# Three joins and one order of tiles in an odd block, and the last attention pair woven with the projection behind it

## The reference

```
z = h @ w_in; u, g = split(z)                       # odd mixer
d = multiscale_pool(u)                              # 4 groups of 512 channels, windows 2, 4, 8, 16
y = einsum("bngi,gij->bngj", d, w_grp) * scale
out = (y * silu(g)) @ w_out

logits = q @ k.T * scale + c[t] - c[s]              # forgetting attention, causal, c = cumsum(log f)
o = softmax(logits) @ v
h = h + (o * silu(g)) @ fox_w_out
```

## Time and profile before

| | us |
|---|---|
| runs | 3169.97, 3166.43, 3172.95; median 3169.97 |
| profiled execution | 3172.45 |
| its span, first to last instruction | 3170.3 |
| TensorE busy | 2962.7 (93%) |
| VectorE, GpSimd, ScalarE busy | 1746.6, 1316.3, 1088.0 |

### The profile page before, as it was taken

The page is one execution under the profiler, slowest core; times in us unless marked ns, Lnnn a source line. Parts: engine busy times, 40 slices in busy tenths (PEclk is TensorE's granted clock), DMA queues, the critical chain, the costliest instruction groups (busy, mean ns, idle before and its releaser), DMA issues.

```text
span 3170.3 us, 40111 instructions
## 1 busy us (share of the span) xinstructions
PE 2962.7 (93%) x13930; PEld 2287.7 (72%) x13930; DVE 1746.6 (55%) x2284; ACT 1088.0 (34%) x1429; POOL 1316.3 (42%) x1638
## 2 busy tenths in 40 slices
PE   5999999989999999989899999998999999997997
PEld 3688888757788777867688877776667666665775
DVE  7688999955545116534632322535555655556353
ACT  5344444342211000001332221324455555665232
POOL 2344454447644434436422324775221121211575
PEclk9999999999999999999899999999999999999999
DMA  7412222344311321113301103333222212221423
GB/s 298 161 63 64 63 76 73 114 151 162 102 49 44 116 80 37 47 39 137 107 27 34 33 27 106 96 87 131 54 47 54 48 33 48 48 34 41 140 82 111
DMA packets 113294, 258.56 MB, mean 82 GB/s; under 512 B 24624, under 2 KB 38000, under 8 KB 112384
## 3 DMA queue, kind: packets, MB, share of 16 engines
q1 hardware_dynamic: 83456, 189.43, 20.5%
q10 hardware_dynamic: 29696, 67.21, 5.9%
HBM read 223.97 MB, written 32.64 MB: 81 GB/s over the span
## 4 chain that ended last, share of the span: by engine, by line
PE 75%; DVE 11%; ACT 6%; POOL 4%; issue 3%; DMA 2%; DVEq 0%; POOLq 0%; SPq 0%; ACTq 0%
PE ps L660 20%; PE ps L661 19%; PE ps L662 19%; POOL t_wl L590 3%; PE ps L1212 2%; PE ps L1229 1%; DVE ps L2117 1%; PE ps L1027 1%; PE ps L1028 1%; PE ps L1029 1%; POOL t_wh L585 1%; DVE t_ptl L2580 1%; PE ps L1249 1%; ACT t_pr L1848 1%; DVE t_pb L2327 1%
## 5 line engine op out<-in xcount | busy, mean ns | idle before, releaser
L660 PE MATMUL ps<-t_h_hi,t_wh 128*128 128x512 f32 x2464 | 1011.6, 411 | 43.9 <-POOLq L593 13.5
L585 POOL CAST t_wh<-t_wst 128x1024 fp32r<-128x1024 f32 (+2 forms) x306 | 313.6, 1025 | 1712.1 <-PE ps L662 1538.9
L661 PE MATMUL ps<-t_h_lo,t_wh 128*128 128x512 f32 x2464 | 982.7, 399 | 0.0
L662 PE MATMUL ps<-t_h_hi,t_wl 128*128 128x512 f32 x2464 | 981.9, 398 | 0.0
L590 POOL TENSOR_TENSOR t_wl<-t_wst,t_wh 128x256 fp32r<-128x256 f32 (+2 forms) x1224 | 926.1, 787 | 24.5
L660 PEld LDWEIGHTS ps<-t_h_hi,t_wh 128*128 128x128 f32 x2464 | 467.8, 190 | 196.7 <-issue 60.5
L661 PEld LDWEIGHTS ps<-t_h_lo,t_wh 128*128 128x128 f32 x2464 | 469.0, 190 | 112.7 <-issue 8.5
L662 PEld LDWEIGHTS ps<-t_h_hi,t_wl 128*128 128x128 f32 x2464 | 467.6, 190 | 112.2
L2117 DVE SCALAR_TENSOR_TENSOR ps<-t_upad,t_vec,ps 128x1024 f32<-128x1024 f32 x224 | 275.5, 1284 | 7.1 <-DVE ps L2111 0.9
L660 PE MATMUL ps<-t_y_hi,t_wh 128*128 128x512 f32 x512 | 208.4, 407 | 21.7 <-DVEq L264 14.6
L661 PE MATMUL ps<-t_y_lo,t_wh 128*128 128x512 f32 x512 | 205.6, 402 | 0.0
(11 more groups left out here) (350 smaller groups left out, 4267.4 us busy)
## 6 DMA issues: line engine op xcount, KB each, us to landing
t_wst<-w_even_in SPq DMA_DIRECT2D x40, 512.0 KB, 3.5
t_wst<-w_ple SPq DMA_DIRECT2D x64, 320.0 KB, 2.9
t_wst<-w_even_out SPq DMA_DIRECT2D x32, 512.0 KB, 3.6
t_wst<-w_fox_in SPq DMA_DIRECT2D x32, 512.0 KB, 3.6
t_modw<-w_mod SPq DMA_DIRECT2D x6, 2048.0 KB, 16.2
t_xr<-x_d ACTq DMA_DIRECT2D x6, 2048.0 KB, 11.6
t_wst<-w_gla_in SPq DMA_DIRECT2D x24, 512.0 KB, 3.8
t_wst<-w_odd_in_a SPq DMA_DIRECT2D x16, 512.0 KB, 3.6
```

What stands on the lines that cost most here:

```text
L585: pool.tensor_copy(wh[b][:, 0:w], wst[b][:, 0:w]).then_inc(S("w_high"), 1)
L660: pe.matmul(o, w1, x1, start=start and k == 0, stop=False)
L661: pe.matmul(o, w1, x2, start=False, stop=False)
L662: last = pe.matmul(o, w2, x1, start=False, stop=stop and k == kts - 1)
```

## The change

In the odd block the tiles 4 to 11 of a group come in another order, gate 0, gate 1, group 0, group 1, then as before (`ODD_ORDER`; loads by `ODD_AT`, widths by `ODD_WIDTHS`). Three `begin` waits of TensorE go: into `oout_a` and `oout_b` it waits for y of tile 6 only (`o_y`), and takes each further step of y as it is ready (`y_ready`); into `odd_b` it waits for the last residual (`x_added`).

In the last attention window VectorE runs `add_scores` of unit i+1 ahead of `low_weights` of unit i. TensorE gets 14 contraction steps (3 matmuls each) of half tiles 0 and 1 of the output projection at steps 9 to 22 (`EARLY`, into banks 6 and 7), the last two behind the window. Their operand, half 0 of `t_yf`, is split by GpSimd (`last_pair`: 8 times a copy and a subtraction of 128x512, each once its pair is done), behind the split of the projection's first two weight tiles; SyncE issues these two loads ahead of the last `load_max`. ScalarE and VectorE split half 1 only, and ScalarE issues the load of x ahead of its copies.

```diff
+ODD_ORDER = [(0, 0), (0, 1), (1, 0), (1, 1), (0, 2), (1, 2), (0, 3), (1, 3)]
...
+        return bank(6 + t if name == "fout" and t < 2 else t % 4)
...
+    EARLY = [(0, 0), (0, 1), (0, 2), (1, 0), (0, 3), (1, 1), (0, 4), (1, 2), (0, 5), (0, 6), (1, 3), (0, 7),
+             (1, 4), (1, 5)]
+    EARLY_AT = {9 + n: x for n, x in enumerate(EARLY)}
...
                     store_max(times - 1, c)
+                    if c == 1:
+                        for j in range(2):
+                            load_tile("w_fox_out", 0, j, j * T, T, (T, T))
                     load_max(times - 1, c)
...
+        def last_pair():
+
+            for i in range(1, 9):
+                if 1 <= i <= 8:
+                    k = i - 1
+                    pool.wait_ge(S("f_y"), 4 * k + 2)
+                    pool.tensor_copy(hcol(h_hi, 0, k), hcol(yf, 0, k)).then_inc(S("yf_high"), 1)
+                    pool.wait_ge(S("yf_high"), k + 1)
+                    pool.tensor_tensor(hcol(h_lo, 0, k), hcol(yf, 0, k), hcol(h_hi, 0, k).bitcast(F32),
+                                       ALU.subtract).then_inc(S("yf_ready"), 1)
...
+        def y_ready(part, k):
+            pe.wait_ge(S("o_gs"), 8 * part + 2 + k + 1)
...
-        begin(pe, "oout_a")
-        out_phase("w_odd_out_a", None, None, "w_odd_in_b")
-        begin(pe, "odd_b")
+        pe.wait_ge(S("o_y"), 4 * 1 + 7)
+        out_phase(0, "w_odd_out_a", "w_odd_in_b")
+        pe.wait_ge(S("x_added"), 2 + KT)
         odd_groups(1)
-        begin(pe, "oout_b")
-        out_by_halves("oout_b", "w_odd_out_b", lambda c: None, (y_hi, y_lo))
+        pe.wait_ge(S("o_y"), 4 * 3 + 7)
+        out_by_halves("oout_b", "w_odd_out_b", lambda c: (lambda k: y_ready(1, k)) if c == 0 else None, (y_hi, y_lo))
...
+        def early_out(t, ks):
+
+            base = first["w_fox_out"]
+            if ks[0] == 0:
+                pe.wait_ge(S("f_g"), 8)
+                pe.wait_ge(S("w_split"), base + t + 3)
+            last = project(wbuf("w_fox_out", t), None, h_hi, h_lo, chunks=[(0, HALF, out_bank("fout", t))], ks=ks,
+                           ready=(lambda k: pe.wait_ge(S("yf_ready"), k + 1)) if t == 0 else None)
+            if ks[-1] == KT - 1:
+                last.then_inc(S("w_used"), 1)
...
+                if attend and not project_more and h in EARLY_AT:
+                    early_out(EARLY_AT[h][0], (EARLY_AT[h][1],))
...
-        begin(pe, "fout")
-        out_by_halves("fout", "w_fox_out", lambda c: lambda k: pe.wait_ge(S("yf_ready"), 8 * c + k + 1), (h_hi, h_lo))
+        early_out(1, (6, 7))
+
+        pe.wait_ge(S("f_add"), 24 * 8)
+        out_by_halves("fout", "w_fox_out", lambda c: lambda k: pe.wait_ge(S("yf_ready"), 8 * c + k + 1), (h_hi, h_lo),
+                      done=2)
...
+                if isinstance(p, int) and p == 7 and i > 1:
+                    act.wait_ge(S("f_pv"), NU * p + i - 1)
                 A(pth[x][:, 0:n], pr[x][:, 0:n], ACT.Copy).then_inc(S("f_ph"), 1)
...
-            at_least("f_pv", NU * p + i - 1)
+            if not (isinstance(p, int) and p == 7):
+                at_least("f_pv", NU * p + i - 1)
+            elif i > 1:
+
+                dve.wait_ge(S("f_pl"), 24 * p + 2 * i - 2)
...
+                    if h % 2 == 1 and not project_more and h < 23:
+                        add_scores(p, h // 2 + 1, like)
                     if h % 2 == 1:
                         low_weights(p, h // 2)
```

More of the change, by code:

```diff
@@ L32 @@
 KB = 1024
+ODD_ORDER = [(0, 0), (0, 1), (1, 0), (1, 1), (0, 2), (1, 2), (0, 3), (1, 3)]
+ODD_AT = [1024 * j for j in range(4)] + [4096 + 1536 * j + 1024 * kind for kind, j in ODD_ORDER]
+ODD_WIDTHS = [1024] * 4 + [(1024, 512)[kind] for kind, j in ODD_ORDER]
 STREAMS = [
@@ L545, in _ @@
             for half in range(passes(name)):
+                if name == "w_fox_out" and half == 0:
+                    with sp.Fori(0, times - 1) as i:
+                        for j, w in enumerate(widths):
+                            load_tile(name, i + 1, j, j * T, w, widths)
+                    continue
                 with sp.Fori(0, times) as i:
                     for j, w in enumerate(widths):
-                        load_tile(name, i, j, sum(widths[:j]) if name != "w_even_in" else EVEN_AT[j], w, widths,
+                        load_tile(name, i, j, ODD_AT[j] if name.startswith("w_odd_in") else sum(widths[:j]), w, widths,
                                   half * times * len(widths))
@@ L624, in _ @@
             for half in range(passes(name)):
+                if name == "w_fox_out" and half == 0:
+                    for j, w in enumerate(widths):
+                        split_tile(name, 0, j, w, widths, 0)
+                    pool.wait_ge(S("w_used"), first[name] + 2)
+                    last_pair()
+                    with pool.Fori(0, times - 1) as i:
+                        for j, w in enumerate(widths):
+                            split_tile(name, i + 1, j, w, widths, 0)
+                    continue
                 with pool.Fori(0, times) as i:
@@ L692, in half_added, with out_by_halves @@
             pe.wait_ge(S("r_added"), 16 * ADD[name] + t + 1)
-        def out_by_halves(name, nm, ready, operand):
+        def out_by_halves(name, nm, ready, operand, done=0):
             base = first[nm]
@@ L699, in out_by_halves @@
                     t = 8 * c + m
+                    if t < done:
+                        continue
                     if t >= 4:
@@ L974, in group @@
                     project(j % 2, slot(j), h_hi, h_lo).then_inc(S("w_used"), 1)
[L975 to L984, removed]
+                for n, (kind, j) in enumerate(ODD_ORDER):
+                    take(nm, i, 4 + n)
+                    if kind == 0:
+                        act((9, 11, 13, 14)[j])
+                        project(n % 2, slot(2 * j % 4), h_hi, h_lo).then_inc(S("w_used"), 1)
+                    else:
+                        act(10) if j == 0 else act(12) if j == 1 else yev(3 + j)
+                        if j == 0:
+                            pe.wait_ge(S("o_d"), 4 * g + 4)
+                        project(n % 2, slot((2 * j + 1) % 4), d_hi, d_lo, kts=4).then_inc(S("w_used"), 1)
             if part == 0:
@@ L1626, in group @@
                 for j in range(4):
-                    act.wait_ge(S("w_used"), w0 + 5 + 2 * j + i * 12)
+                    act.wait_ge(S("w_used"), w0 + 5 + ODD_ORDER.index((0, j)) + i * 12)
                     act.wait_ge(S("o_gs"), 4 * g + j + 1)
@@ L1910, in _ @@
         begin(act, "fout")
-        for c in range(2):
-            for k in range(KT):
-                A(hcol(h_hi, c, k), hcol(yf, c, k), ACT.Copy).then_inc(S("yf_high"), 1)
         load_x(x_d)
+        for k in range(KT):
+            A(hcol(h_hi, 1, k), hcol(yf, 1, k), ACT.Copy).then_inc(S("yf_high"), 1)
         act.wait_ge(S("yf_ready"), 16)
@@ L2342, in odd_groups @@
                 for j in range(4):
-                    dve.wait_ge(S("w_used"), w0 + 6 + 2 * j)
+                    dve.wait_ge(S("w_used"), w0 + 5 + ODD_ORDER.index((1, j)))
                     dve.wait_ge(S("o_act"), 8 * g + 13 + j)
@@ L2605, in window @@
             for h in range(24):
-                if attend and h % 2 == 0:
+                if attend and h % 2 == 0 and (project_more or h == 0):
                     add_scores(p, h // 2, like)
@@ L2643, in _ @@
         begin(dve, "fout")
-        for c in range(2):
-            for k in range(KT):
-                n = 8 * c + k + 1
-                dve.wait_ge(S("yf_high"), n)
-                TT_(hcol(h_lo, c, k), hcol(yf, c, k), hcol(h_hi, c, k).bitcast(F32), ALU.subtract)\
-                    .then_inc(S("yf_ready"), 1)
+        dve.wait_ge(S("yf_ready"), 8)
+        for k in range(KT):
+            dve.wait_ge(S("yf_high"), 9 + k)
+            TT_(hcol(h_lo, 1, k), hcol(yf, 1, k), hcol(h_hi, 1, k).bitcast(F32), ALU.subtract)\
+                .then_inc(S("yf_ready"), 1)
         out_by_halves("fout", "w_fox_out", lambda k: V("ple_norm", 8 + k), lambda: p_split(1))
```

16 lines of the change are left out of this document (7 added, 9 removed).

## The result

The changed kernel takes 3137.59 us (median of 4, 3135.76 to 3139.97) against 3171.46 of the kernel before in the same job; the ratio is 0.9896, 95% interval 0.9879 to 0.9913. It is 34 us faster where the forecast was 48: the sign holds, but the time lies outside the forecast's own range of 3115 to 3129, at the upper edge of the wide one (3108 to 3138), and it is what the rival "the window gets much longer" said (3138).

What follows compares the result with a forecast made beforehand. TensorE was taken as the bound, busy 2962.7 of 3170.3 us, so only its waits and slow-clock stretches could be won. Odd block 39 plus last pair 9 (18.5 - 1.3 - 8) gave 48 off: 3122 against the median, range 3115 to 3129.

Steps and rivals of the forecast that it cites:

- the window gets much longer: Last pair, rival: TensorE drops to its lower clock at each unit's pause; pair gives -7, total 3138; chance 0.17.
- Odd block, 39: Odd block: shorter waits and slow stretches at joins and groups win 39 us, bounds 30 to 43.
- The margin of 0.2 at the split of gate 2: Odd block, first two groups: GpSimd's split, 5.4 us, fits group tile 1's 5.6, four times; 1.0 taken off.
- Last pair, what goes, 18.5: Last pair: wait of 6.29, slow stretch of 2.4 and 9.8 of steps moved into gaps, together 18.5 us.
- x late: Output projection: x's residual ready at 13.9, half tile 4 wants it at 12.6, so 1.3 us come back.
- Window longer by 8: Last pair's window: adds ahead and the first projection step lengthen it by 8 us in all.
- the ring: Last window: low part, values, scores, add follow one another, 5.3 us per full unit against a chain of 3.9.
- The first half: Window up to low part 4: 5 to 7 us later, 6 taken, through the first projection step waiting for GpSimd.
- The second half: Window from low part 4 to low part 11: 30.4 us against 28.7, so 2 more.
- Window shorter: Last window, rival: a unit costs only VectorE's busy 2.7 us, not 3.9; 6 us less, total 3108; chance 0.12.
- Odd block in part: Odd block, rival: VectorE's chain longer, or x or gate 2's split late; 39 becomes 25, total 3136; chance 0.14.
- slower: Last pair, rival: GpSimd's eight copies and subtractions hold TensorE, 85 us in place of 18; total 3189; chance 0.02.

Runs made afterwards that it cites:

- own low buffers: Changed kernel with first two weight tiles loaded early, TensorE's scores also a unit ahead, and low parts in separate buffers: 3117.9 us, ratio 0.9835 to the kernel before.
- The kernel with adds alone: Odd block changed; in the last pair only VectorE's scores added a unit ahead, no projection steps or GpSimd copies: 3154.1 us, ratio 0.9943 to the kernel before.
- weights early: Changed kernel with the output projection's first two weight tiles asked for ahead of both stores of maxima: 3132.5 us, ratio 0.9878 to the kernel before.
- steps with weights early: Changed kernel with scores added in their old place and first two weight tiles loaded ahead of the maxima: 3125.7 us, ratio 0.9862 to the kernel before.
- x early: Changed kernel with old add order, first two weight tiles loaded early, and half 0 of x loaded during the last window: 3122.4 us, ratio 0.9844.

## Why the forecast was right and wrong, step by step

**Odd block, 39: right**, 37.2 measured (34.5 in the kernel with it alone). Joins are 17.9 by the profile and 21 by the time for 18.2, the order of tiles 19.3 and 15 for 20.9: the sum stands firmer than its two parts. The waits that stay are 1.9 and 3.3 for 1.5 and 2.7. The margin of 0.2 at the split of gate 2 held: TensorE's longest wait for GpSimd in the block is 1.8 us, as it was in the kernel before.

**Last pair, what goes, 18.5: right.** With x early and the residual ahead the tail is 17.6 shorter.

**"x late", 1.3: too small, and half of the mechanism.** The wait is 4.0 us and followed by matmuls of 0.80 us. The load of x started 5.3 us behind the last values as forecast (5), but landed 9.6 later and not 8.2, which by the working above makes 3 of the 4.0. The last 1 is a wait that the forecast did not have: residual 0 is queued behind eight low parts of half 1 on VectorE, 8.8 us. The change had moved the eight of half 0 away but left these in front, while TensorE now arrives early. Each of the two hides behind the other, so taking x away alone gave 1.9; both together are worth 5 of the 17 (tail 227.1 with own low buffers, 221.9 with both taken away as well).

**Window longer by 8: the step that failed.** Measured 16.7. The main fault is the price of the ring, which was worked out at full clock. Where TensorE has its full clock the ring of 5.3 per full unit stands in the trace, at 5.3 to 5.5. But with adds ahead TensorE waits in each of the first three units (5.23, 1.90, 2.07) and for GpSimd (2.96), and stands at 0.50 for 29.7 us in place of parts of 22 us in the kernel before, and two stretches of its work, values and scores, lie in the ring. The kernel with adds alone shows it bare: 74.4 us, 7.2 per unit. I had priced the low clock only in a rival.

The first half, forecast at 6, is 11.3 longer, and has two paths of nearly the same length. On the path that the forecast took, the first step came 26.9 us into the window for 24.7 (weights at 14.0 for 10.4, splits and copy a little faster), low part 4 followed 5.8 behind it for 4.3, at low clock, and 1.4 had been rounded away (6 for 7.4). This path would have been late at full clock too. The other is the slow ring, which makes low part 4 as late with no late step at all (31.9 with weights early). The second half, forecast at 2 longer, is 5.3 longer. Of the 3.3 missed, 2.6 are the one unit of 8.2 for 5.6: values and scores took 4.15 (2878.17 to 2882.32) for 2.56 at the low clock, and low part 4 took 2.68 beside GpSimd for 1.6. So the low clock is one of several causes in the changed kernel. Taking away one of the two paths leaves a window of 62.6 or 64.5, taking away both leaves 54.4.

By the forecast's terms TensorE's idle time in the window would fall by 1.8 us (8 longer, with 9.8 of work in it). It rose by 1.3, and fell, to 8.9, in the kernel with the ring opened.

**The rival "much longer" was right in mechanism, and in its time partly by luck**: -7 for the pair, about -5 measured, 3138 for 3137.6. Its window was 24 longer (8, 8, 5 and 3) where 16.7 were measured, and its tail 17.2 shorter where it was 12.1: two misses of 7 and 5 that nearly cancel. It had TensorE drop in every unit, and the last ones ran at full clock. Of its terms the 3 for waiting is the 2.96 measured, and GpSimd's contention, 5, is about 2.6 (low parts 2, 3 and 4 take 1.45, 1.58 and 2.68 us, and 0.76, 0.49 and 1.82 with the odd block alone); the rest is ring and low clock. The Trainium skill (TensorE: Matmul & The Clock Gate, A second HAM failure mode: psum-queue depth-cycling) tells of short pauses between groups of matmuls that make the clock swing between its two levels and cost throughput. The traces agree on the cost, though with the clock staying low and not swinging, for pauses of 2.7 us at 7.2 us per unit (0.50 for 45 us) and do not for pauses of 1.1 to 1.3 at 5.3 us per unit (1.00 for 29 us).

**"Window shorter" was wrong for the reason given against it**, the ring; with the ring opened it came true in part (48.8 us with 14 steps inside, 2.7 shorter and not 6, as TensorE's own work then sets 3.6 to 4.0 per unit). "Odd block in part" and "slower" did not happen.

## What to carry to other kernels

Before an operation is put a unit ahead on one engine, write down the whole loop through every engine that feeds it and every buffer it writes: running ahead on one side only closes a new ring. Price such a ring at the clock that the pauses in it leave, not at full clock, since TensorE's own part of it takes twice as long at half clock. Check that work moved into gaps makes the idle time smaller. And when work is moved away from the front of a phase, look what is left in front of the first result that the other engine will now want earlier, and list everything that ends there within a microsecond: taking away one of two such waits shows only a part of what both are worth.

## What was not expected of the hardware

The lower clock stayed through a loop of pauses: with a pause of 2.7 us in every unit the granted clock was 0.50 for 45.6 us and 0.59 over the 19.8 behind them; with two more steps of work in the same gap it was back at 1.00 for the last 29 us of the window.

The first matmul behind a wait does not tell whether the clock falls. In the kernel with own low buffers a wait of 4.02 us in the projection was followed by a first matmul of 0.50 us, and 0.8 us later the matmuls were slow:

```profile
2904.70 0.50 PE L706 MATMUL ps<-t_h_hi,t_wh 128*128 128x512 f32 x1 [4.02 <-DVE t_xr L2318]
...
2905.91 0.63 PE L707 MATMUL ps<-t_h_lo,t_wh 128*128 128x512 f32 x1
```

Nor does the length of a wait tell how long the slow stretch is. Waits of 4.02, 4.00, 3.17 and 2.50 us (own low buffers, changed, steps with weights early, x early) were followed by slow matmuls up to 4.2, 5.3, 5.7 and 3.5 us behind the restart. What decides it stays open.
